# Most of each output projection summed under the last group of attention heads

## The reference, cut to what matters

```python
h = modulate(rms_norm(x, norm_g[layer, 1]), mod[:, 1, 0], mod[:, 1, 1])
y = mixer(h, ...)            # attention over 16 heads -> (512, 1024), then  @ w_o  (1024 x 1024)
x = x + mod[:, 1, 2][:, None, :] * y
h = modulate(rms_norm(x, norm_g[layer, 2]), ...)      # needs all of the new x
```

## Time and profile before

| | us |
|---|---|
| median of 3 runs (lowest to highest) | 2625.91 (2622.34 to 2627.13) |
| the profiled execution | 2623.75 |
| its span, first to last instruction | 2622.0 |
| TensorE matmul busy | 2452.5 (94%) |
| DVE busy | 1366.8 (52%) |
| ACT busy | 872.6 (33%) |
| mean granted TensorE clock | 0.961 of full |

### The profile page before, as it was taken

How to read it: one execution, slowest core, us unless ns; L and a number is a source line. 1 busy time by engine, 2 the same in 40 slices (tenths; PEclk the granted TensorE clock), 3 DMA queues, 4 the chain that set the end, 5 groups by cost and what they waited for, 6 DMA issues and landing times. The chain is left out here.

```text
span 2622.0 us, 34645 instructions
## 1 busy us (share of the span) xinstructions
PE 2452.5 (94%) x12230; PEld 2069.9 (79%) x12230; DVE 1366.8 (52%) x2010; ACT 872.6 (33%) x1212; POOL 133.6 (5%) x125
## 2 busy tenths in 40 slices
PE   2999998999889999999999999998899979899998
PEld 1888886887778888879998888886688877788886
DVE  6555445566555554454445555445567665433333
ACT  2333223344433332232223333222344443333321
POOL 2000000111000000001111000000111100000000
PEclk9999998999589999989999999999899989899999
DMA  6555432655235554335556555435777881232332
GB/s 227 185 190 186 142 118 86 201 170 174 82 113 193 190 188 131 120 106 183 188 182 211 193 188 187 130 122 149 190 214 222 224 206 61 75 97 97 97 97 85
DMA packets 133919, 406.43 MB, mean 155 GB/s; under 512 B 16720, under 2 KB 17104, under 8 KB 133712
## 3 DMA queue, kind: packets, MB, share of 16 engines
q1 hardware_dynamic: 120784, 355.06, 44.4%
q0 software_dynamic: 13056, 50.33, 5.1%
HBM read 352.90 MB, written 52.43 MB: 155 GB/s over the span
## 5 line engine op out<-in xcount | busy, mean ns | idle before, releaser
L256 PE MATMUL ps<-h_hi,w_hi 128*128 128x512 f32 x2048 | 818.6, 400 | 40.1 <-DVE h_lo L590 25.0
L251 DVE TENSOR_TENSOR w_lo<-w_raw,w_hi 128x1024 fp32r<-128x1024 f32 (+1 forms) x384 | 470.8, 1226 | 685.1 <-ACT w_hi L247 685.0
L257 PE MATMUL ps<-h_lo,w_hi 128*128 128x512 f32 x2048 | 808.4, 395 | 0.0
L258 PE MATMUL ps<-h_hi,w_lo 128*128 128x512 f32 x2048 | 808.1, 395 | 0.0
L247 ACT CAST w_hi<-w_raw 128x1024 fp32r<-128x1024 f32 (+1 forms) x384 | 395.0, 1029 | 836.8 <-PE ps L258 834.1
L256 PEld LDWEIGHTS ps<-h_hi,w_hi 128*128 128x128 f32 x2048 | 392.0, 191 | 131.6 <-issue 41.6
L258 PEld LDWEIGHTS ps<-h_hi,w_lo 128*128 128x128 f32 x2048 | 390.9, 191 | 83.6
L257 PEld LDWEIGHTS ps<-h_lo,w_hi 128*128 128x128 f32 x2048 | 391.9, 191 | 77.2
L256 PE MATMUL ps<-act_hi,w_hi 128*128 128x512 f32 x704 | 275.5, 391 | 0.0
L258 PE MATMUL ps<-act_hi,w_lo 128*128 128x512 f32 x704 | 274.1, 389 | 0.0
L257 PE MATMUL ps<-act_lo,w_hi 128*128 128x512 f32 x704 | 274.0, 389 | 0.0
(11 more groups left out here) (80 smaller groups left out, 2357.2 us busy)
## 6 DMA issues: line engine op xcount, KB each, us to landing
w_raw<-gate_up SPq DMA_DIRECT2D x176, 512.0 KB, 3.7
ada_raw<-ada SPq DMA_DIRECT2D x160, 512.0 KB, 4.5
w_raw<-down SPq DMA_DIRECT2D x80, 512.0 KB, 3.6
w_raw<-kv_w SPq DMA_DIRECT2D x48, 512.0 KB, 3.6
w_raw<-mixa_w SPq DMA_DIRECT2D x32, 512.0 KB, 3.8
w_raw<-mixb_w SPq DMA_DIRECT2D x32, 512.0 KB, 3.6
kb<-rot_st POOLq DMA_DIRECT2D x12, 1024.0 KB, 5.1
vb<-v_out POOLq DMA_DIRECT2D x12, 1024.0 KB, 4.9
```

The lines of the kernel that those rows point to most:

```text
L251: eng.tensor_tensor(w_lo[:, slot, 0:n], w_raw[:, slot, 0:n], w_hi[:, slot, 0:n].bitcast(F32), ALU.subtract).then_inc(w_lo_done[slot], 2)
L256: nc.tensor.matmul(out_ap, l_hi, r_hi, start=start, stop=False, skip_group_check=skip)
L257: nc.tensor.matmul(out_ap, l_hi, r_lo, start=False, stop=False, skip_group_check=skip)
L258: return nc.tensor.matmul(out_ap, l_lo, r_hi, start=False, stop=stop, skip_group_check=skip)
```

## The change

The sum over channel tiles is cut in two. The first six tiles come from the three earlier groups and are there when the last group begins (tile 5 just then). For each of the eight tiles of y, the product over these six (`OUT_K = 6`) is made by 24 parts of six matmuls, `pe_out_part`, three parts a tile. They stand between the steps of the last group: two a step in steps 2 to 11, one a step in steps 12 to 15. DVE adds each finished tile of y to `x` with the gate (`dve_out_add`). The rounding and remainder of the six tiles is placed in steps 0 to 2, two a step; that of tile 6 in step 13. The other two channel tiles follow (`pe_out_tail`): tile 6 for four of the y tiles during the last two weighings, tile 7 and the rest after the last transpose. The last channel tile is read straight from PSUM, without the copy to `att`. Each y tile is then added to `x` a second time, squared and summed, one at a time.

Weights: units 24 to 31 hold six tiles' worth each (768 elements used), units 32 and 33 the two remaining tiles for four y tiles each, so ten units take the place of eight. SP loads them between the heads' loads.

```diff
-PHASES = (..., ("mixA", 24), ("woA", 8), ... ("mixB", 24), ("woB", 8), ...)
+PHASES = (..., ("mixA", 24), ("woA", 10), ... ("mixB", 24), ("woB", 10), ...)
+OUT_K = 6
+OUT_N = OUT_K * P
+OUT_SUBSTEPS = {step: (2 * step - 4, 2 * step - 3) for step in range(2, 12)} | {step: (step + 8,) for step in range(12, 16)}
+OUT_HIGH = {3: 2, 4: 3, 6: 4, 7: 5, 9: 6, 10: 7, 13: 8}
+OUT_LOW = {4: 2, 5: 3, 7: 4, 8: 5, 10: 6, 11: 7, 14: 8}
+OUT_ADD = {3: 0, 5: 1, 6: 2, 8: 3, 9: 4, 11: 5, 12: 6}
+OUT_IN = {0: (0, 1), 1: (2, 3), 2: (4, 5), 13: (6,)}
+TAIL_BANK = (0, 1, 2, 6)
...
+        def pe_out_part(pe, name, n):
+            tile, u0 = n // 3, UNIT0[name]
+            if n % 3 == 0:
+                out_unit_ready(pe, name, tile)
+                if tile < 3:
+                    pe.wait_ge(pair_free, PAIR0[name] + 2)
+                else:
+                    pe.wait_ge(part_added, (0 if name == "woA" else KT) + tile - 2)
+            for k in (n % 3 * 2, n % 3 * 2 + 1):
+                if tile == 0:
+                    pe.wait_ge(h_lo_done, h_count(name) + k + 1)
+                cols = slice(k * P, (k + 1) * P)
+                mm = three_passes(ps[:, tile % 3, :], w_hi[:, tile % 2, cols], w_lo[:, tile % 2, cols],
+                                  h_hi[:, k, :], h_lo[:, k, :], k == 0, k == OUT_K - 1)
...
+        def pe_out_tail(pe, name, tile, k):
+            slot, c = tile // 4, (tile % 4 * 2 + k - OUT_K) * P
+            if k == OUT_K:
+                if tile % 4 == 0:
+                    out_unit_ready(pe, name, 8 + slot)
+                if tile == 0:
+                    pe.wait_ge(h_lo_done, h_count(name) + OUT_K + 1)
+                if tile < 4:
+                    pe.wait_ge(part_added, (0 if name == "woA" else KT) + (7, 8, 6, 0)[tile])
+                else:
+                    pe.wait_ge(x_first, X_FIRST[name] + tile - 3)
...
-            group(None, G - 1, None)          # TensorE
+            for s in range(STEPS):
+                subs = OUT_SUBSTEPS.get(s, ())
+                score(a, s)
+                if s == 11:
+                    transpose_o(a, 0)
+                for n in subs[:1]:
+                    pe_out_part(pe, wo, n)
+                if s >= 1:
+                    transpose_p(a, s - 1)
+                for n in subs[1:]:
+                    pe_out_part(pe, wo, n)
+                if s >= 2:
+                    weigh_v(a, s - 2)
+            transpose_p(a, 15)
+            weigh_v(a, 14)
+            for tile in range(3):
+                pe_out_tail(pe, wo, tile, OUT_K)
+            weigh_v(a, 15)
+            pe_out_tail(pe, wo, 3, OUT_K)
+            transpose_o(a, 1)
+            for tile in range(4):
+                pe_out_tail(pe, wo, tile, KT - 1)
+            for tile in range(4, KT):
+                for k in (OUT_K, KT - 1):
+                    pe_out_tail(pe, wo, tile, k)
...
-            group(None, G - 1, False, True, False)          # DVE
+            for s in range(STEPS):
+                negated_max(a, s)
+                if s in OUT_LOW:
+                    dve_out_low(dve, wo, OUT_LOW[s])
+                if s >= 1:
+                    split_pt(a, s - 1)
+                for k in OUT_IN.get(s, ()):
+                    dve_out_in(dve, wo, k)
+                if s >= 2:
+                    o_scale(a, s - 2)
+                if s in OUT_ADD:
+                    dve_out_add(dve, wo, OUT_ADD[s])
+            split_pt(a, 15)
+            o_scale(a, 14)
+            dve_out_add(dve, wo, 7)
+            o_scale(a, 15)
+            dve_out_low(dve, wo, 9)
...
+        def dve_out_tail(dve, name, r):
+            dve_out_in(dve, name, KT - 1, ps[:, OT_BANK[name[-1]], :])
+            sum_clear(dve, r)
+            for n in range(KT):
+                # wait for tile n of TensorE
+                nc.vector.scalar_tensor_tensor(out=x[:, n, :], in0=ps[:, TAIL_BANK[n % 4], :], ...)
+                if n >= 1:
+                    add_square(n - 1)
+                if n == 5:
+                    w_split_lo(dve, u0 + 10, 0)
+            add_square(KT - 1)
+            w_split_lo(dve, u0 + 11, 1)
...
-            group(None, G - 1, False, True)          # SP
-            for j in range(28, 32):
-                w_dma(sp, u0 + j, j % 2, weights[j])
+            for j, after_q, after_v in ((0, (28,), ()), (1, (29,), (30, 31)), (2, (32,), (33,))):
+                load_k(sp, layer, a, j + 1)
+                load_q(sp, layer, a, j + 1)
+                if j > 0:
+                    for n in after_q:
+                        w_dma(sp, u0 + n, n % 2, weights[n])
+                load_v(sp, layer, a, j + 1)
+                for n in after_v if j > 0 else after_q:
+                    w_dma(sp, u0 + n, n % 2, weights[n])
```

More of the change, by code:

```diff
@@ L1039, in split @@
                     if gemm:
-                        w_split_hi(act, g * 6 + u0 + j, j % 2)
+                        out = isinstance(g, int) and g * 6 + j >= 6 * G
+                        w_split_hi(act, g * 6 + u0 + j, j % 2, OUT_N if out else UNIT)
                 if not attend:
@@ L1075, in act_mixer @@
             group(G - 1, G - 2, True, True, False)
-            group(None, G - 1, False, True, False)
[L1078 to L1095, removed]
@@ new lines, in act_mixer, with out_view, act_out_in, act_out_high @@
+            act_out_last(act, wo)
+        def out_view(name):
+            return by_class if name == "woA" else classes
+        def act_out_in(act, name, k):
+            if k == 0:
+                act.wait_ge(unit_used, UNIT0[name])
+            if k >= OUT_K - 1:
+                act.wait_ge(att_done, (0 if name == "woA" else KT) + k + 2)
+            nc.scalar.copy(classes(h_hi[:, k, :]), out_view(name)(att[:, k, :])).then_inc(h_hi_done, 1)
+        def act_out_high(act, name, n):
+            w_split_hi(act, UNIT0[name] + n, n % 2, OUT_N if n < 8 else UNIT)
@@ L1149, in split @@
                     if gemm:
-                        w_split_lo(dve, g * 6 + u0 + j, j % 2)
+                        out = isinstance(g, int) and g * 6 + j >= 6 * G
+                        w_split_lo(dve, g * 6 + u0 + j, j % 2, OUT_N if out else UNIT)
                 if not attend:
@@ L1188, in dve_mixer @@
             group(G - 1, G - 2, True, True, False)
-            group(None, G - 1, False, True, False)
+            wo, a = "wo" + name[-1], G - 1
+            dve.wait_ge(mod_ready, g_block + 1)
+            nc.vector.tensor_scalar(g_col[:], mod[:, g_block, :], 1.0, None, ALU.mult).then_inc(col_ready, 1)
+            dve.wait_ge(col_ready, col_n)
+            for s in range(STEPS):
+                negated_max(a, s)
+                if s in OUT_LOW:
+                    dve_out_low(dve, wo, OUT_LOW[s])
+                if s >= 1:
+                    split_pt(a, s - 1)
+                for k in OUT_IN.get(s, ()):
+                    dve_out_in(dve, wo, k)
[8 more added lines that the diff above has]
+            dve_out_low(dve, wo, 9)
         def pool_mixer(pool, name):
@@ L1405, in pack_tiles, with pack_out @@
     return np.stack([pack_pair(w[:, j * P:(j + 1) * P]) for w in pairs for j in range(2)])
+def pack_out(w):
+    parts = [np.pad(pack_pair(w[:OUT_N, n * P:(n + 1) * P]), ((0, 0), (0, UNIT - OUT_N))) for n in range(KT)]
+    tails = [np.concatenate([pack_pair(w[OUT_N:, n * P:(n + 1) * P]) for n in range(4 * m, 4 * m + 4)], axis=1)
+             for m in range(2)]
+    return np.stack(parts + tails)
 def rotary_columns(w):
@@ L1439 @@
     down = down.reshape(4, FT, P, 4, PAIR).transpose(0, 3, 2, 1, 4).reshape(4, 4, P, FT * PAIR)
-    def out_pairs(w):
-        return [w[:, n * PAIR:(n + 1) * PAIR] for n in range(4)]
     def group_columns(w, g):
```

100 lines of the change are left out of this document (80 added, 20 removed).

## The result

The changed kernel takes 2599.93 us (median of four runs, 2598.41 to 2601.42), the kernel before 2624.12 in the same session (four runs, 2618.69 to 2627.13). The ratio is 0.9905, with an interval of 0.989 to 0.992: faster by some 24 us. The forecast was 2603.

A forecast was written before the change was run, and what follows sets the result against it. Both places were taken as TensorE-bound or nearly so, layer 0 at a low clock. Layer 0 +20.2-36.4 = -16.2, layer 1 +28.9-36.1 = -7.2, together -23.4 us: forecast 2603, range 2590 to 2615.

The forecast's parts named there:

- The path: Both layers: last group, transpose of the last channel tile, projection, statistics; -16.2 us in layer 0, -7.2 in layer 1.
- Start of the group: Steps 0 to 2: input roundings and remainders delay step 3's maximum, +8.6 us in layer 0, +3.3 in layer 1.
- cheap start and end: Rival, 13%: input tiles hide in TensorE's pauses and the eighth addition is early; -35.5 us, 2590.
- Steps: Last group's middle: two-part steps of 5.70 us in layer 1, about 4 in layer 0, from TensorE's sum.
- 12.3 steps of attention and 21 parts: Layer 0 after step 3's maximum: TensorE has 15.1 us of attention, 28.6 of parts, 0.5 of transpose.
- End of the group: Last probability transposes to last channel tile's transpose: 6.9 us in layer 0, 7.8 in layer 1, 2.1 from new waits.
- Tail: Last channel tile's transpose to statistics: 16.7 us against 53.1 in layer 0, 15.9 against 52.0 in layer 1.
- A stays at 1.2 GHz: Rival, 6%: layer 0's last group stays at the low clock despite the parts; slower, 2645 us.
- Weights late: Rival, 4%: weights arrive late, a 1.5 us pause for each of 16 y tiles; 2627 us, no change.
- Steps longer: Rival, 17%: some 25 filled steps exceed TensorE's sum by 0.30 to 0.5 us each; 2610 to 2615 us.
- No overlap: Rival, 2%: parts wait for all attention, so only the tail gains; about 2620 us.

The follow-up runs named there:

- class-order run: Changed kernel, with layer 0's copy from PSUM to att writing class order, so roundings and remainders read att without a stride: 2595.09 us, ratio 0.9882.
- the run with everything a step later: Changed kernel with three mends (class-ordered copy, earlier last weighing, later unit remainders), plus input remainders, parts, units and additions one step later: 2590.77 us, ratio 0.9856.
- the order run: Changed kernel, with channel tile 6's matmuls for y tile 1 moved behind the last weighing, in both layers: 2596.36 us, ratio 0.9888.
- the 96 idle matmuls: Kernel before the change, with six unused 512-column matmuls added to each of 16 steps of layer 0's last group: 2631.59 us, ratio 1.0023.
- the thin parts: Changed kernel, with one matmul instead of six in each of the 24 parts of both projections, waits kept: 2578.07 us, ratio 0.9811.
- layer 0 alone: The change made in layer 0 only, layer 1's projection as in the kernel before: 2613.63 us, ratio 0.9944.

## Why the prediction was right

**The path, right.** Group plus tail is the whole difference, and nothing is given back behind it: between the statistics of A and the first score of B lie 1360.25 us, before 1361.73. This holds for a profile of before with the faster course in B, from which the forecast too was worked out; against one with the slower course the difference would be some 6 us more.

**Start of the group, right in kind, 0.7 too long.** Three gaps of 4.5 were forecast for A; they are 3.85, 4.14 and 5.00, and the class-order run shows that the strided inputs are in them: with cheaper remainders the maximum of step 3 comes 2.5 earlier. B: 14.34 against a sum of 14.9. That this was a term that slack might hide (the rival *cheap start and end*) is half right: a mend of the inputs gave 3.1 of the 8.6, one of the order 1.5 a layer. But the run with everything a step later shows the limit of it: a start that is 4 us shorter because parts were moved out of it comes back in the middle, where TensorE is full.

**Steps, right in B, too cheap in A.** B's two-part steps take (2166.88-2121.88)/8 = 5.63 from the maximum of step 3 to that of step 11, with TensorE busy for all of the 45.00 us, and 5.73 from step 4 to step 12, against 5.70. (The one step from 3 to 4, which stands in the sum as 4.6 without a working, took 5.42.) A's take 4.03, against 2.59+1.36 = 3.95: the halved 1.2 GHz step was a good price. From the maximum of step 3 to the last transposes A took 47.57 where the prediction has 44.2. The term that failed is "12.3 steps of attention and 21 parts" as a sum of TensorE's work alone in steps 12 to 14: 9.70 instead of 7.77. There DVE stands for 1.47 waiting for ACT's rounding of tile 6, then takes the remainder (719.96), and `o_scale` behind it holds the weighing of 721.82. With the rounding a step earlier and the remainder right behind the maximum the same steps took 8.15. The prediction put the seventh input, in step 13, into DVE's total but at nothing on the path; by that run it cost 1.6 us. Another 1.5 us more than forecast lie in the eight two-part steps and the last round together; the last round, from the maximum of step 15 to its transposes, took 1.76, with the pause of 0.88 for ACT's exponentials in it. The start (-0.7) and the end (-0.3) take back part of it, so the group is 2.4 longer than forecast (68.00 against 65.6).

**End of the group, right.** 6.59 for 6.9 and 7.69 for 7.8. The mechanism (weighing behind tile 1, tile 1 behind the eighth addition) is in the rows, and the order run took it away.

**Tail, too long in A by 2.0, right in B.** From L525 to the first matmul 2.06 instead of 3.0, from there to the first addition 1.0 instead of 1.1, and to the statistics 11.7 instead of 12.5: 14.75 for 16.7. Of the first, 0.8 is the strided read from PSUM, priced at 1.03 on each engine by the row of SBUF; it took 0.586 on ACT and 0.691 on DVE, as in B without a stride. The Trainium skill (SBUF — State Buffer, "Door 1: The DMA port swizzle") gives PSUM smaller cachelines than SBUF and warns of non-contiguous access there for matmuls. Carried over to ACT and DVE, as the prediction did, that pointed the other way: neither these rows nor the copies of the class-order run, 586 ns with and without a stride, bear it out. The third is DVE's price: 0.71 was the length of one instruction in a merged row, 1.42 for the two of a tile, while from start to start a tile takes 1.26. In B the low clock hides this: the clock is 0.70 over the first 5.6 us of the tail, the first two additions wait for TensorE (1.11 and 0.53), and 15.84 meets 15.9 by two errors that cancel; where the clock stayed up, in the class-order run, B's tail took 14.77.

**Rivals.** *A stays at 1.2 GHz*: refuted, 2.4 from 673.89, 9.4 us after the start, and 1.00 in every stretch from 675 to 732, so it did not keep falling and rising either; the 96 idle matmuls show that the dense work alone does it. *Weights late*: no wait of TensorE for `w_lo` or keys in either group (only the 3.07 for the queries at B's first score, as before); the thin parts point to the loads as the next bound in B. *Steps longer*: in A's steps 12 to 14 (3.23 against 2.59), elsewhere by about 0.1. *No overlap*: refuted by the stretches. Two errors of +2.4 and -2.0 in A cancel, so a sum of 82.3 met 82.75; the total, -22.5 against -23.4, is better than its terms.

## What to carry to other kernels

Where an engine is nearly full at a lowered clock, its busy share hides free capacity: 21.8 us of dense matmuls cost 3.3 there. When work moves under another stage, list every instruction of it with the queue and the step where it lands: the one input tile put at nothing on the path was the largest error in the group. And read for each engine what stands behind a waiting instruction: moving one waiting tile behind the last weighing was worth 1.5 us a layer, while bringing a maximum forward by moving the remainders behind it was worth nothing, since TensorE's order still held the next step behind a part that waited for them.

## What the runs showed of the hardware

- Reading every fourth element of 4 bytes cost ACT and DVE nothing from PSUM (586 and 691 ns for 128x512 in A, with the stride, and in B, without), while from SBUF a strided pair of remainders takes 2.06 to 2.12 us and a contiguous one 1.29.
- The same code with the same inputs starts B's last group at 2.4 GHz after 6.6 us in one profile and stays at 1.2 GHz for over 20 in others (before, against the runs with idle matmuls and with layer 0 alone), with TensorE fully busy with the attention's own matmuls in the meantime (5.00 of 5.00 us in the stretch from 2125); the difference is 4 to 6 us. It fits the spread of before (2619 to 2631 over 14 runs), wider than the 2 to 4 us over four runs each of the kernels that make all the parts in both layers; but the latter are fewer runs, no pair of profiles of one kernel shows both courses, and what decides between them is open.
- The clock can stay low although TensorE is nearly full: 0.50 for the 45 us of A's last group before, with TensorE busy for 40.0. With 96 products of 512 columns among the same work it rose 5.2 us after the first score.
